# Output gate load ahead of the S5 store, keys turned ahead of the scores, transpose banks per tile, streamed buffers at multiples of 64 bytes

## What is computed

```python
for layer in range(DEPTH):                       # DEPTH = 2
    mixed = even_mixer(h, ...) if layer % 2 == 0 else odd_mixer(h, ...)
    h = layer_norm(ALPHA * h + mixed @ w_out[layer], ln1_w[layer], ln1_b[layer])
    ffn = moe(h, router_w[layer], router_bias[layer], exp_w_gate[layer], exp_w_up[layer], exp_w_down[layer], ...)
    h = layer_norm(ALPHA * h + ffn, ln2_w[layer], ln2_b[layer])

def even_mixer(x, w_in, ...):
    q, k, v, o, g, xb, gb = jnp.split(x @ w_in, EVEN_SPLITS, axis=-1)
    y_a = head_norm(mlstm(q, k, v, ...), norm_w, True) * jax.nn.sigmoid(o)
    y_b = rglru(xb, gb, conv_w, conv_b, wa, ba, wx, bx, lam)

def gla(q, k, v, log_alpha, r, norm_w):          # by chunks of 64 tokens
    q_dec = qc * jnp.exp(bcum)
    k_inv = kc * jnp.exp(-bcum)
    k_end = kc * jnp.exp(b_last - bcum)
    u = jnp.einsum('bhnld,bhnle->bhnde', k_end, vc)
    att = jnp.where(causal, jnp.einsum('bhnid,bhnjd->bhnij', q_dec, k_inv), 0.0)
```

## Time and profile before

| what | us |
|---|---|
| median of three executions | 1309.98 |
| profiled execution, its own time | 1309.92 |
| its span, first to last instruction | 1308.2 |
| TensorE busy | 1281.9 (98%) |
| VectorE busy | 529.7 (40%) |
| ScalarE busy | 188.9 (14%) |
| GpSimd busy | 46.8 (4%) |
| transfers, mean over the span | 353 GB/s |
| granted TensorE clock, mean | 0.991 |

### The profile page before, as it was taken

One profiled execution on the slowest core, in us unless ns is written; L12 is line 12 of the kernel. 1 busy time (PEld: TensorE's weight loads), 2 busy tenths in 40 slices (PEclk: granted clock), 3 DMA queues, 4 the chain that ended last, 5 costly groups with the idle time before them and its releaser, 6 DMA issues.

```text
span 1308.2 us, 17012 instructions
## 1 busy us (share of the span) xinstructions
PE 1281.9 (98%) x6761; PEld 694.0 (53%) x6761; DVE 529.7 (40%) x1073; ACT 188.9 (14%) x315; POOL 46.8 (4%) x76
## 2 busy tenths in 40 slices
PE   9989999999999999999999999999999999999997
PEld 7864654454445544454487656544455444544443
DVE  6794633333333333333327146233333333333324
ACT  3231201111111111111122212111111111111111
POOL 6200100000000000000010001000000000000000
PEclk9999999999999999999999899999999999999999
DMA  8864959999999999999943069599999999999992
GB/s 261 234 226 169 407 214 403 422 421 422 422 422 422 423 421 422 421 422 422 368 169 130 28 267 390 219 415 422 421 422 421 422 422 421 422 422 422 422 421 113
DMA packets 77625, 462.33 MB, mean 353 GB/s; under 512 B 9680, under 2 KB 10896, under 8 KB 27152
## 3 DMA queue, kind: packets, MB, share of 16 engines
q1 hardware_dynamic: 77584, 461.74, 87.1%
HBM read 455.36 MB, written 6.36 MB: 353 GB/s over the span
## 4 chain that ended last, share of the span: by engine, by line
PE 91%; DVE 4%; DMA 3%; ACT 1%; issue 0%; SPq 0%; DVEq 0%; ACTq 0%
PE bank L1062 34%; PE bank L1094 18%; PE bank L992 10%; PE bank L1013 9%; PE bank L635 3%; PE bank L621 3%; PE bank L965 2%; PE bank L685 2%; PE bank L699 2%; DMA weight_ring<-in_w_in_even 1%; PE bank L1073 1%; DMA expert_weights<-s_rows 1%; PE bank L1001 1%; PE bank L1027 1%; DMA s_rows<-hidden 1%; PE bank L796 1%
## 5 line engine op out<-in xcount | busy, mean ns | idle before, releaser
L1094 PE MATMUL bank<-expert_weights,hiddenT 128*64 128x512 f32 x1024 | 233.8, 598 | 0.0
L1062 PE MATMUL bank<-expert_weights,hT 128*64 128x512 f32 x1024 | 225.3, 592 | 0.0
L1062 PE MATMUL bank<-expert_weights,weight_ring 128*64 128x512 f32 x1024 | 225.2, 592 | 0.0
L1843 DVE TENSOR_TENSOR hidden<-silu_gate,bank 128x256 f32<-128x256 f32 x64 | 27.0, 422 | 329.9 <-ACT silu_gate L1285 329.9
L1062 PEld LDWEIGHTS bank<-expert_weights,weight_ring 128*64 128x64 f32 x1024 | 73.6, 137 | 146.2 <-issue 146.2
L1062 PEld LDWEIGHTS bank<-expert_weights,hT 128*64 128x64 f32 x1024 | 73.4, 137 | 145.3 <-issue 145.0
L1094 PEld LDWEIGHTS bank<-expert_weights,hiddenT 128*64 128x64 f32 x1024 | 67.8, 136 | 118.3 <-issue 110.0
L1013 PE MATMUL bank<-onehot_r,h_top 128*128 128x256 f32 x512 | 125.5, 288 | 0.0
L1013 PE MATMUL bank<-onehot_r,h_low 128*128 128x256 f32 x512 | 119.7, 277 | 0.0
L992 PE MATMUL bank<-y_top,onehotT_r 128*128 128x512 f32 x264 | 112.1, 425 | 0.0
L992 PE MATMUL bank<-y_low,onehotT_r 128*128 128x512 f32 x264 | 104.5, 396 | 0.0
(11 more groups left out here) (361 smaller groups left out, 1071.4 us busy)
## 6 DMA issues: line engine op xcount, KB each, us to landing
expert_weights<-in_exp_w_gate SPq DMA_DIRECT2D x128, 1024.0 KB, 11.1
expert_weights<-in_exp_w_up SPq DMA_DIRECT2D x128, 1024.0 KB, 13.9
expert_weights<-in_exp_w_down SPq DMA_DIRECT2D x128, 1024.0 KB, 13.2
weight_ring<-in_w_in_even SPq DMA_DIRECT2D x6, 2048.0 KB, 13.1
weight_ring<-in_w_out SPq DMA_DIRECT2D x4, 2048.0 KB, 8.1
weight_ring<-in_w_in_odd SPq DMA_DIRECT2D x4, 2048.0 KB, 10.2
s_c<-expert_weights SPq DMA_DIRECT2D x1, 3072.0 KB, 9.7
expert_weights<-s_c SPq DMA_DIRECT2D x1, 3072.0 KB, 11.2
```

The source lines that it names most:

```text
L1062: last_mm = nc.tensor.matmul(bank[6][a * CAP:(a + 1) * CAP, :].rearrange("p (w f) -> p w f", w=2), xq[:, c, s0:s0 + CAP], ew_gu(2 * u + a, c),
L1094: last_mm = nc.tensor.matmul(bank[b][a * CAP:(a + 1) * CAP, :], hm[:, j, a * CAP:(a + 1) * CAP], ew_d(2 * u + a)[:, j, half * 512:(half + ...
L1843: nc.vector.tensor_tensor(hslot[:, :], sg[:, :], bank[6][:, DE:2 * DE], ALU.mult)\
```

## The change

It makes four edits. In `sp_mix0`, o0's `ring_load` moves ahead of the waits and the store of `s5_c`. In mix1, TensorE turns the keys before the scores, and ScalarE copies keT, then att, then does gelu. At each stage start, banks T0 and T1 (4 and 5) take tile 0, T2 and T3 (6 and 7) tile 1, four channel blocks each; ScalarE copies T0, T1 and T2 and VectorE only T3 (in mix0 the split stays T0, T2 and T1, T3). In the MoE stages the matmuls between the tiles are ten of 128 columns on `ident` instead of five of 256 on hT. Last, `slot_gate` is laid behind `y_top`, so that the buffers from `gathered_xT` to `y_top` begin at multiples of 64.

```diff
@@ -128,7 +128,6 @@
         onehotT = nc.alloc_sbuf_tensor_at("onehotT_r", [P, 2, TT, P], FR, offset=onehotT_at)
-        slot_gate = sb("slot_gate", [P, 2])
         xg = sb("gathered_xT", [P, KC, 2 * CAP])
@@ -153,6 +152,7 @@
         y_top = nc.alloc_sbuf_tensor_at("y_top", [P, D], FR, offset=y_top_at)
+        slot_gate = sb("slot_gate", [P, 2])
         wsum = sb("wsum", [P, TT])
@@ -332,10 +332,11 @@
             sp.dma_start(A["s5_b"], s5_room[:, 0:4096]).then_inc(M1["stored"], 16)
+            ring_load(sp, ring_no["o0"])
             sp.wait_ge(M1["tables"], 1)
             sp.wait_ge(M1["ct"], 1)
             sp.dma_start(A["s5_c"], s5_room[:, 6144:12288]).then_inc(M1["stored"], 16)
-            for name in ("o0", "out_b0", "out_a0"):
+            for name in ("out_b0", "out_a0"):
@@ -467,10 +468,10 @@
-        odd_jobs = [("T0", "a"), ("T1", "d"), ("T2", "a"), ("T3", "d"), ("low", "a"), ("u0", "a"), ("u1", "a"),
+        odd_jobs = [("T0", "a"), ("T1", "a"), ("T2", "a"), ("T3", "d"), ("low", "a"), ("u0", "a"), ("u1", "a"),
...
-                    ("v0", "a"), ("v1", "a"), ("y0", "d"), ("r0", "a"), ("y1", "d"), ("att0", "a"), ("att1", "a"),
-                    ("keT", "a"), ("U0", "d"), ("U1", "d"), ("U2", "d"), ("r1", "a"), ("gl0", "a"), ("gl1", "a"),
+                    ("v0", "a"), ("v1", "a"), ("y0", "d"), ("r0", "a"), ("y1", "d"), ("keT", "a"), ("att0", "a"), ("att1", "a"),
+                    ("U0", "d"), ("U1", "d"), ("U2", "d"), ("r1", "a"), ("gl0", "a"), ("gl1", "a"),
@@ -651,6 +652,10 @@
+        def turned_rows(i):
+
+            return hT[:, 4 * (i % 2):4 * (i % 2) + 4, (i // 2) * P:(i // 2 + 1) * P]
+
@@ -658,15 +663,14 @@
-                for b in range(4):
-                    for c in (2 * b, 2 * b + 1):
-                        last = nc.tensor.transpose(B.tile(f"T{b}")[:, (c % 2) * SEQ + t * P:(c % 2) * SEQ + (t + 1) * P],
-                                                   h[:, t, :].rearrange("p (q c) -> p c q", c=KC)[:, c, :],
+                for b in range(2):
+                    for c in range(4):
+                        last = nc.tensor.transpose(B.tile(f"T{2 * t + b}")[:, c * P:(c + 1) * P],
+                                                   h[:, t, :].rearrange("p (q c) -> p c q", c=KC)[:, 4 * b + c, :],
                                                    ident[:, :])
-                    if t == TT - 1:
-                        last.then_inc(B.full_sem, 1)
+                    last.then_inc(B.full_sem, 1)
@@ -923,21 +927,20 @@
                 if t:
-                    keep_clock(pe, 0, 5)
+                    warm_up(pe, 0, 10)
                 wait_h(pe, f"moe{l}", t)
...
+                    last.then_inc(m["tD"] if t and b else m["tA"], 1)
@@ -1196,8 +1205,8 @@
             B = B1
-            act_copies(act, B, "T0", hT[:, 0:2, :])
-            act_copies(act, B, "T2", hT[:, 4:6, :])
+            for i in range(3):
+                act_turned(act, B, f"T{i}")
@@ -1586,9 +1602,7 @@
             B = B1
-            wait_h(dve, "mix1")
-            for row in (1, 3):
-                dve_copies(dve, B, f"T{row}", hT[:, 2 * row:2 * row + 2, :])
+            dve_turned(dve, B, "T3")
```

More of the change, by code:

```diff
@@ L604, in _, with warm_up @@
                     pool_moe(pool, int(st[-1]))
-        def warm_up(pe, count):
+        def warm_up(pe, b, count):
             for _ in range(count):
-                nc.tensor.matmul(bank[7][:, 0:P], ident[:, :], ident[:, :], start=True, stop=True)
+                nc.tensor.matmul(bank[b][:, 0:P], ident[:, :], ident[:, :], start=True, stop=True)
         def keep_clock(pe, b, count):
@@ L851, in pe_mix1 @@
             pe.wait_ge(*B.read("qk1"))
+            B.wait_free(pe, "keT")
+            for pr in range(2):
+                for t in range(TT):
+                    last = nc.tensor.transpose(B.tile("keT")[:, (2 * pr + t) * P:(2 * pr + t + 1) * P],
+                                               W["ke"][:, pr, t * P:(t + 1) * P], ident[:, :])
+            last.then_inc(B.full_sem, 1)
             for hh in range(2):
@@ L860, in pe_mix1 @@
                 last.then_inc(B.full_sem, 1)
-            B.wait_free(pe, "keT")
-            for pr in range(2):
-                for t in range(TT):
-                    last = nc.tensor.transpose(B.tile("keT")[:, (2 * pr + t) * P:(2 * pr + t + 1) * P],
-                                               W["ke"][:, pr, t * P:(t + 1) * P], ident[:, :])
-            last.then_inc(B.full_sem, 1)
             pe.wait_ge(*B.read("keT"))
@@ L1118, in _ @@
             pe.wait_ge(S["consts"], 1)
[L1119 removed]
+            warm_up(pe, 7, 10)
             pe.wait_ge(S["consts"], N_CONSTS)
@@ L1133, in act_copies, with act_turned @@
             nc.scalar.copy(dst, B.tile(name)[:, :].rearrange("p (a t) -> p a t", a=2)).then_inc(B.done["a"], 1)
+        def act_turned(act, B, name):
+            i = int(name[1])
+            act.wait_ge(*B.full(name))
+            nc.scalar.copy(turned_rows(i), B.tile(name)[:, :].rearrange("p (c t) -> p c t", c=4)).then_inc(B.done["a"], 1)
         def act_mix0(act, chain):
             B = B0
-            act_copies(act, B, "T0", hT[:, 0:2, :])
-            act_copies(act, B, "T2", hT[:, 4:6, :])
+            act_turned(act, B, "T0")
+            act_turned(act, B, "T2")
             act.wait_ge(*B.read("gates"))
@@ L1237, in act_mix1 @@
                 last.then_inc(B.done["a"], 1)
-            act_copies(act, B, "keT", W["ke_tok"])
+            act.wait_ge(*B.read("y1"))
+            nc.scalar.activation(W["gT"], W["gT"], ACT.Gelu_apprx_tanh).then_inc(M1["gelu5"], 1)
             act.wait_ge(*B.full("r1"))
@@ L1258, in act_moe @@
             m = MO[l]
-            for i, b in enumerate((0, 2)):
+            for i in range(3):
                 act.wait_ge(m["tA"], 1 + i)
-                nc.scalar.copy(hT[:, 2 * b:2 * b + 2, :], bank[4 + b][:, :].rearrange("p (c t) -> p c t", c=2))\
+                nc.scalar.copy(turned_rows(i), bank[4 + i][:, :].rearrange("p (c t) -> p c t", c=4))\
                   .then_inc(m["hT_a"], 1)
@@ L1349, in dve_copies, with dve_turned @@
             nc.vector.tensor_copy(dst, B.tile(name)[:, :].rearrange("p (a t) -> p a t", a=2)).then_inc(B.done["d"], 1)
+        def dve_turned(dve, B, name):
+            i = int(name[1])
+            dve.wait_ge(*B.full(name))
+            nc.vector.tensor_copy(turned_rows(i), B.tile(name)[:, :].rearrange("p (c t) -> p c t", c=4))\
+              .then_inc(B.done["d"], 1)
         def dve_mix0(dve, chain):
             B = B0
-            for i, row in enumerate((1, 3)):
-                dve_copies(dve, B, f"T{row}", hT[:, 2 * row:2 * row + 2, :])
+            for i in (1, 3):
+                dve_turned(dve, B, f"T{i}")
             nc.vector.memset(V["xbp"][:, :, 0:3], 0.0)
```

31 lines of the change are left out of this document (12 added, 19 removed).

## The result

The changed kernel takes **1299.43 us** (median of four, 1298.43 to 1300.64) against 1309.74 for the kernel before beside it: a ratio of 0.9919, with a 95% interval from 0.9907 to 0.993. It is faster, by 10.3 us, where 15.8 were forecast, and lies 1.4 us above the end of the range. The profiled execution took 1300.64 us, its span is 1298.9 (before 1308.2), so the profile shows 9.3 us of gain.

A forecast was written before the change was run, and what follows sets the result against it. The prediction took TensorE's chain as the bound, with a few waits and half-clock stretches, and expert-loop transfers as a close second limit. Gains of 7.5 + 6.17 + 0.6 + 1.5 = 15.8 us from 1309.92 gave 1294.1 us, range 1290.5 to 1298.0.

The forecast's parts named there:

- Step 1: Even mixer (mix0): o0 loaded ahead of the S5 store lands at 84.4, so o no longer waits; 7.5 us.
- 4.98 + 2.52 us: mix0's o matmuls: 4.98 us from starting earlier, 2.52 us from running without the lower clock.
- Step 2: Odd mixer (mix1): keys turned and copied before the scores remove 2.87 us of wait and 3.30 us of half clock; 6.17 us.
- 0.44 us behind them: mix1 before the change: the scores were said to take 0.44 us behind the turned keys, ending at 733.09.
- Step 3: Stage starts: one copy per engine left after the second tile's transposes; 0.19 us at three stages, 0.6 us together.
- Step 4: Expert loops: aligned y_top and y_low make scatter matmuls 4 to 15 ns faster; 1.5 us kept over both layers.
- The cap of step 4: Expert loops: transfers need 14.91 us a pair, so a faster scatter is worth hardly more than 1.0 to 1.9 us.
- (a): Scatter: alignment gives nothing, its spacing is its own; 1295.6 us, chance 0.22.
- (f): Expert pair: moved buffers make writes and array reads meet, lengthening the scatter; slower if over 0.25 us a pair; chance 0.02.
- (c): MoE stages: the router's clock fall vanishes, 1292.6 us, or also comes at the earlier stage, 1295.6; chance 0.18 either way.
- (d): Mixers: one wait goes but its clock fall stays, 3.3 or 2.5 us less gain; 1297.4 us at most, chance 0.09.
- (e): mix0: o0 lands no earlier because another load or the store holds the engines; 1301.6 us, chance 0.01.

The follow-up runs named there:

- part 1: Kernel before with only o0's load moved ahead of the s5_c store: 1303.25 us, ratio 0.9952.
- part 3: Kernel before with only the turned h's banks changed, a bank for each half of a tile, in all four stages: 1307.52 us, ratio 0.9979.

## Why the prediction failed, step by step

**Step 1 (o0) was right in its mechanism, and its size was one case of two.** o starts within 0.2 us of the last N matmul and takes 13.73 us at full clock, as forecast; o0 lands at 87.0, not 84.4. But 4.98 + 2.52 us holds only when the clock doesn't fall at 58 us. When it does, 4.4 us are left, since the wait had been hiding that fall. The changed kernel's profiled execution had the fall, and its first load landed 0.6 us later: 5.3. The medians, which mix both cases, gave 6.2 for the part alone.

**Step 2 (the keys) was right**: 6.6 us in the profile, 6.2 in the medians, for 6.17. Its "0.44 us behind them" fits no row: by the earlier trace rows the scores end at 732.50 and the keys at 733.09. The sum doesn't use it.

**Step 3 (a bank per tile) was right in the trace**: 0.15 to 0.23 us at a stage for 0.19. Timeline of the changed kernel, second tile of moe0:

```profile
143.39 1.16 PE L934 MATMUL bank<-ident,h 128*128 128x128 f32 x8 [1.48 <-DVE h L1353]
...
144.14 0.58 ACT L1270 COPY hT<-bank 128x512 f32<-128x512 f32 x1 [2.36 <-PE bank L934]
...
144.58 0.69 DVE L1803 COPY hT<-bank 128x512 f32<-128x512 f32 x1 [1.25 <-PE bank L934]
```

The last copy ends at 145.27, 1.88 us behind the first transpose, for 1.85. By the medians the part alone is worth 2.7 us, 1.6 at least. A higher clock would account for 1.6 of the 2.7; the cause of the excess stays open.

**Step 4 (the places) failed, and it is more than the whole miss.** It was given +1.5 us and took 4.9: 1299.43 against 1294.56 with slot_gate back. That is 6.4 us for a miss of 5.3; the other three parts brought 1.0 more than forecast. The sentence that failed is "If alignment is what separates them, a scatter matmul gives back 4 to 15 ns: 0.03 to 0.12 us a pair, 1.0 to 3.8 us a layer; if not, nothing." Its lower bound was zero, though nothing in the profile excluded a loss, and it took the spacing for a property of the operand's address. The runs showed that the gather has two spacings on the same addresses. The 113.8 of the earlier trace rows was the fast one, not a norm that the scatter falls short of, and moving all the buffers together put the gather into the slow one in every pair (2004 to 2060 ns) and lengthened the scatter (1968 to 1992). Which buffers do it together is shown above in part, how they do it isn't. The prediction's own sign for wrong altogether, a pair over 14.8, is what came. The part of step 4 that could be had, y_top aligned by itself, is 17 ns a pair, inside the 4 to 15 ns a matmul that I gave its four.

The cap of step 4, transfers that hold back a faster pair, never came into play. Its pace was right: in the first layer the up-weights of successive pairs land 14.91 us apart in the trace of before and 14.92 at a pair of 14.77. What it missed is that the head start differs from trace to trace: at 14.77 the loads near the loop's start landed after 13.8 us instead of 15.2, those of the last pairs after 17.2 to 17.8, and over a microsecond was left. With a pair of 14.87 the last pair's landed after 15.2.

The Trainium skill, "SBUF — State Buffer", Specifications (TRN2), gives SBUF lines of 16 bytes. By that alone a shift of 32 bytes, a multiple of 16, would change nothing and part 4 would be 0; the runs disagree with it as with me: 0.082 us a pair.

**The rivals.** (a), alignment gives nothing, has the right sum of the three other parts: 1295.6 for a measured 1294.56 without the move. That it is so near is in part luck: timed alone, part 1 gave 1.3 us less than forecast and part 3 2.1 more. (f) was the right place and the right sign for part 4, and I priced it wrongly: it stood in the text as a case that decides at 0.25 us a pair and lies at 0.35, with 0.02. At the measured 0.08 it costs 5.2 us, which is far from slower than before but enough to leave the range. Its mechanism, writes that meet reads, isn't shown: in the changed kernel the slow spacing goes on to 452.41 us, while VectorE is idle from 451.71, and a small matmul ahead lifts it in every second pair. (c), a clock fall elsewhere, came both ways: the router's fall of 1.4 us was gone at moe1, and the one at 58 us was there; among the profiled executions each comes and goes. (d) and (e) didn't happen.

Had the unknown of step 4 been bounded below by as much as above, 3.8 us a layer, the range would have reached 1295.6 + 7.6 = 1303.2 and held the result.

## What to carry to other kernels

A spacing of matmuls read at one place of a trace is not that instruction's speed; look for the same instruction elsewhere in the trace, as in the opening gathers here, before a gain is built on the difference. An edit that moves many buffers for the sake of one should be cut to the one, and its unknown bounded on both sides of zero. And a wait that a change removes may have been hiding something that comes and goes from execution to execution: its gain is then two numbers, and one profile shows only one of them.

## What the hardware showed that I had not expected

- The 256-column fp32r matmuls of the gather go on at either 113 or 118 ns from start to start, on the same addresses. In all 20 traces, those entered with 200 to 203 ns from the first to the second start stay at 116 ns or more for two steps at least, many to the end; those entered with 205 to 208 are at 113 or 114 after one step more at most. What chooses is not settled: moving silu_gate and hidden by 32 bytes changes it in every second pair, y_top on top of all the others in every pair, a 32-column matmul ahead in every second pair, their own order not at all.
- The 512-column ones of the scatter have, behind the first, steps of 224 to 240 ns, and the order in which y_top and y_low take turns moves them by 53 ns over eight matmuls.
- The granted clock falls to 0.50 at the same few places of the program, at each in some executions and not in others: at 58 us in 10 of 20 profiled executions, for 3.4 us, and so with one and the same kernel. At the very end it is at 0.50 in all 20.
- Whether silu_gate or hidden is the one, and how these or y_top reach a matmul that touches none of them, wasn't tried further and stays open.
